# A two-block model on one core: where ScalarE loads the logarithm's tables, who scales the last rows and columns, and the order of the side work

## The chip, the cores and the metric

The kernel runs on one core of a Trainium2 chip. The metric is the device time of one execution, in microseconds (us); before the change it is 1814.29 us, the median of three executions (1814.15 to 1815.69).

## What is computed

`reference()` runs two small transformers one after the other on 256 tokens of width 1024, batch 1, in fp32.

- The first has two layers. Layer 0 mixes with four heads of differential attention and four heads of a gated linear recurrence; layer 1 mixes with 16 heads of dilated attention. Each layer then has a layer norm ("ln1"), a feed-forward part of width 4096 with a squared relu, a second layer norm ("ln2"), and a gated embedding.
- The second has two layers on a main path (x, the output of the first) and on a context path (256 context tokens). Each layer has an RMS norm with a modulation, a mixer of three parts (gated linear attention, six heads of neighbourhood attention, six heads of sliding-window attention; both attentions of the main path see 512 keys, the context's 256), a gated residual, a second modulated RMS norm, and a SwiGLU of width 2816. The context path ends with the keys and values of layer 1.
- The last step is an RMS norm, and that is what the change touches at the end:

```python
def rms_norm_2(x, g):
    xf = x.astype(jnp.float32)
    y = xf * lax.rsqrt(jnp.mean(xf * xf, axis=-1, keepdims=True) + NORM_EPS)
    return (y * g.astype(jnp.float32)).astype(x.dtype)
...
    return rms_norm_2(x, final_norm)
```

## The kernel before

Activations lie transposed: 128 partitions by 8 chunks (`DC`) of the width, each chunk 256 tokens. A product of weights and activations is done in three matmuls per 128x128 block (L620 to L622, or L660 to L662 where weights are the moving side): every fp32 operand is split into a high part (rounded by ScalarE) and a low part (the rest, by VectorE), and high x high, high x low and low x high are summed in a bank of PSUM.

**Weights** come in three streams from one array in HBM, loaded by SyncE (L564). "main" has 410 tiles of 8 blocks for the first model and the main path, "side" has 110 tiles for the context path, "mod" has 96 tiles for the modulations (L820). Main and side tiles are cut into halves of 4 blocks (128x512). ScalarE makes the high part of a half tile (L586: `high<-ring`, `high_side<-ring_side`), VectorE the low part (L594). The side's ring has 4 halves.

**Order.** Every engine runs a fixed list of instructions. `Program.run` writes these lists in advance: each stage is a generator that yields the name of what it needs next, each lane (engine) keeps a clock of estimated times (`A_us`, `V_us`, ...), and of the parts that can go on first on a lane the one with the lowest rank is taken. TensorE's side and modulation parts have a rank that changes with time (`Pace`): `MOD_PLAN` and `SIDE_PLAN` are lists of (TensorE's clock in us, tiles that should be done by then), in between linear. A part that is behind its plan comes first (rank -3 or -6), one that is not comes after the main path (3 or 5) and fills the time in which the main path cannot go on. So the estimated costs and the two plans together set the order of everything.

**Tables on ScalarE.** `Program.tables` (L466) loads a set of activation tables when the next function isn't in the set that is loaded by then: logarithm and exponential are in one set, tanh is in another with the exponential, silu in a third. Squares, copies and scalings need none. A reciprocal root is Ln and then Exp (`rstd`, L868: the load at L470, Ln at L874, Exp at L878).

**Norms.** `scalar_layer_norm` (L1317) squares eight centred chunks (L1322), TensorE sums them over partitions (L1312), then comes `rstd`. In the second model `scalar_square_sums` (L1877) squares each chunk behind its last residual (L1871 on VectorE, squares at L1887), VectorE adds the squares (L1898), TensorE averages over partitions (L1909), and `scalar_rstd` follows. This second form is used on the main path for the feed-forward norms of both layers, for the mixer's norm of layer 1 and for the last norm, and on the context path for the two norms behind its first.

**The end.** `vector_final` (L2528) makes y in eight VectorE instructions, one for each chunk: X times the norm's weight (a column) times the reciprocal root (L2532). `sync_stores` (L2536) stores each chunk, 128 KB, when it is made (L2540).

**Softmax.** A unit is one head; it has two rows of scores (the two halves of the queries). VectorE adds the bias and takes the row's extreme (L1038), ScalarE takes the exponential and its sum (L1107), VectorE inverts the sums (L1072) and scales both rows (`vector_normalise`, L1078), TensorE turns them (`tensor_turns`, L980), VectorE or ScalarE copies the turned blocks (L1058), TensorE multiplies by the values (L1005). Rows have up to 256 columns in the first model (`odd_scores`; `da_scores` of the differential attention aside), 256 in the context (`c_scores`), 512 on the main path (`x_scores` in layer 0, `x_late_T` in layer 1).

Of the kernel before, what the change touches and what calls it, by code (L numbers as in the profile page):

```python
# [16 lines left out]
P = 128  # L17
# [255 lines left out]
def A_us(n):  # L273
    return 0.2 + n / 1200.0


def V_us(n):
    return 0.15 + n / 960.0
# [6 lines left out]
class Program:  # L285
    def __init__(self, nc, ctx, io):
# [17 lines left out]
        self.s_turned_a = signal("turned_copied_scalar")  # L304
# [659 lines left out]
def tensor_turns(k, w, tag, units, banks, Tt):  # L964
    nc, T = k.nc, k.T
    for i, u in enumerate(units):
        blocks = blocks_of(u, Tt[i % len(Tt)])
        for j in range(len(u["rows"])):
            T.wait_ge(k.s_scaled, (yield tag, "scaled", i, j))
# [92 lines left out]
def vector_normalise(k, w, tag, u, i, Tt):  # L1062
# [9 lines left out]
    nc.vector.reciprocal(rd[:, 0:n_rows], den[:, 0:n_rows]).then_inc(*V.tick(k.s_vec, 0.17))  # L1072
    V.wait_ge(k.s_vec, V.last)
    h = n_rows // 2 if u["diff"] else n_rows
    for j in range(h):
        _, _, cols, to, _, _, _ = rows[j]
        names = [] if u["diff"] else [(tag, "scaled", i, j)]
        nc.vector.tensor_scalar(T_[:, to:to + cols], T_[:, to:to + cols], rd[:, j:j + 1], None, ALU.mult).then_inc(  # L1078
            *V.tick(k.s_scaled, V_us(cols) * 0.8, *names))
# [12 lines left out]

def scalar_attention(k, w, tag, units, Tt, PT):
# [3 lines left out]
    for step in range(n + lag):  # L1097
        if step < n:
# [218 lines left out]
def scalar_layer_norm(k, w, tag, b, layer):  # L1317
    nc, A = k.nc, k.A
    for i in range(DC):
# [3 lines left out]
            *A.tick(k.s_squares, A_us(SEQ), (tag, "square", i)))  # L1323
    A.wait_ge(k.s_sums, (yield tag, "summed", DC - 1))
# [552 lines left out]
def scalar_square_sums(k, w, prod, tag):  # L1877

    nc, A = k.nc, k.A
    for i in range(DC):  # L1880
# [4 lines left out]
        else:  # L1885
            j = k.sq_of[tag, i] = yield from w.sq.take(A, (tag, "added", i))
            nc.scalar.activation(w.SQ[:, j, 0:SEQ], w.X[:, i, :], ACT.Square).then_inc(  # L1887
                *A.tick(k.s_squares, A_us(SEQ), (tag, "square", i)))

# [638 lines left out]
def vector_final(k, w):  # L2528
    nc, V = k.nc, k.V
    for i in range(DC):  # L2530
        V.wait_ge(k.s_rstd, (yield ("final",), "rstd"))
        nc.vector.scalar_tensor_tensor(k.y[:, i, :], w.X[:, i, :], k.col("final", i), w.RS[:, 0, 0:SEQ], ALU.mult,  # L2532
                                       ALU.mult).then_inc(*V.tick(k.s_vec, V_us(SEQ), ("y", i)))


def sync_stores(k):  # L2536
    nc, D_ = k.nc, k.D
    for i in range(DC):
        D_.wait_ge(k.s_vec, (yield "y", i))
        nc.sync.dma_start(k.io["out"][:, i, :], k.y[:, i, :]).then_inc(*D_.tick(k.s_out, 0.1, by=16, later=2.0))  # L2540
    D_.wait_ge(k.s_out, D_.last)
# [80 lines left out]
MOD_PLAN = [(0, 0), (115, 20), (195, 32), (390, 76), (435, MOD_TILES)]  # L2622
SIDE_PLAN = [(430, 0), (560, 11), (715, 23), (790, 42), (970, 51), (1035, 72), (1215, 81), (1290, 98), (1375, 100), (1495, 110)]


def emit(k):
# [120 lines left out]
    k.add(V, vector_final(k, x), 0)  # L2747
    k.add(D_, sync_stores(k), 0)
# [231 lines left out]
```

## Time and profile before

| | |
|---|---|
| median of three executions | 1814.29 us (1814.15 to 1815.69) |
| the profiled execution, its own time | 1817.45 us |
| its span (first to last instruction) | 1816.2 us |
| instructions | 37913 |
| mean granted clock of TensorE | 0.991 of full speed |

The profile comes from one more execution, 3.2 us above the median; its span is 1.25 us shorter than its own time. Times in the trace are counted from the span's start. PE is TensorE's matmuls, PEld its weight loads, DVE VectorE, ACT ScalarE, POOL GpSimd, SPq SyncE's queue that issues DMAs. Matmuls overlap one another, so their durations say less than the distance of their starts.

### The profile page before, as it was taken

What the parts mean: (1) busy time and instruction counts of PE and PEld (TensorE: products, weight loads), DVE (VectorE), ACT (ScalarE), POOL (GpSimd) and SP (SyncE); (2) the same over time, 40 slices, a digit from 0 to 9 for tenths busy, and PEclk for the clock granted to TensorE, in tenths of its full rate; (3) what the DMA queues carried; (4) which work ended last, traced back from release to release, by engine and by line L of the source; (5) the groups of instructions that cost most, each with busy time, mean ns of one, the idle gap of its engine ahead of it and who ended that gap; (6) DMA issues with size and microseconds to landing.
All of it is one profiled execution on the core that took longest, in us unless ns stands there. A gap on an engine that the chain in (4) does not pass through costs nothing.

```text
span 1816.2 us, 37913 instructions
## 1 busy us (share of the span) xinstructions
PE 1777.4 (98%) x14762; PEld 1656.5 (91%) x14762; DVE 1352.7 (74%) x2948; ACT 1090.3 (60%) x2317; POOL 78.5 (4%) x81
## 2 busy tenths in 40 slices
PE   9999999999999999999999999999999999999997
PEld 7787999988989999999989998899999998689997
DVE  7676757578888876886687777886876888877766
ACT  5674646477666655665675656565664765565554
POOL 0001100020001000000020010100000000100000
PEclk9999999999999999999999999999999999999999
DMA  9959766886444645456555554456666543245663
GB/s 361 352 163 340 257 189 222 286 318 197 146 139 145 187 145 175 129 168 184 172 158 163 159 152 127 123 164 185 186 189 188 164 146 117 77 140 181 187 183 112
DMA packets 168610, 334.83 MB, mean 184 GB/s; under 512 B 19296, under 2 KB 21152, under 8 KB 168304
## 3 DMA queue, kind: packets, MB, share of 16 engines
q1 hardware_dynamic: 166752, 327.30, 56.6%
q0 software_dynamic: 1680, 5.11, 1.0%
q8 instruction: 117, 1.92, 0.4%
q14 instruction: 61, 0.50, 0.1%
HBM read 331.29 MB, written 1.05 MB: 183 GB/s over the span
## 4 chain that ended last, share of the span: by engine, by line
PE 92%; DVE 3%; DMA 2%; ACT 2%; issue 1%; SPq 1%; ACTq 0%; DVEq 0%
PE bank L620 25%; PE bank L621 24%; PE bank L622 24%; PE bank L1005 2%; PE bank L955 2%; PE bank L660 2%; PE bank L662 2%; PE bank L661 2%; PE bank L820 2%; PE bank L980 2%; PE bank L1312 1%; DMA ring_side<-in_stream 1%; DMA ring<-in_stream 1%; DVE Xx L1345 1%; PE bank L1990 1%
## 5 line engine op out<-in xcount | busy, mean ns | idle before, releaser
L594 DVE TENSOR_TENSOR low<-ring,high 128x512 fp32r<-128x512 f32 x820 | 556.2, 691 | 187.3 <-ACT high L586 176.6
L586 ACT CAST high<-ring 128x512 fp32r<-128x512 f32 x820 | 503.2, 619 | 311.5 <-PE bank L622 252.6
L620 PE MATMUL bank<-XHx,high 128*128 128x256 f32 x1720 | 502.2, 292 | 9.9 <-DVE XLx L1350 2.4
L621 PE MATMUL bank<-XLx,high 128*128 128x256 f32 x1720 | 485.6, 282 | 0.0
L622 PE MATMUL bank<-XHx,low 128*128 128x256 f32 x1720 | 484.9, 282 | 0.0
L620 PEld LDWEIGHTS bank<-XHx,high 128*128 128x128 f32 x1720 | 326.2, 190 | 31.7 <-issue 12.8
L621 PEld LDWEIGHTS bank<-XLx,high 128*128 128x128 f32 x1720 | 326.9, 190 | 0.9
L622 PEld LDWEIGHTS bank<-XHx,low 128*128 128x128 f32 x1720 | 326.7, 190 | 0.0
L586 ACT CAST high_side<-ring_side 128x512 fp32r<-128x512 f32 x220 | 135.2, 618 | 78.8 <-DMA ring_side<-in_stream 73.8
L594 DVE TENSOR_TENSOR low_side<-ring_side,high_side 128x512 fp32r<-128x512 f32 x220 | 152.5, 702 | 37.5 <-ACT high_side L586 32.6
L620 PE MATMUL bank<-XHc,high_side 128*128 128x256 f32 x608 | 176.6, 291 | 3.0 <-DVE low_side L594 3.0
L621 PE MATMUL bank<-XLc,high_side 128*128 128x256 f32 x608 | 172.1, 283 | 0.0
L622 PE MATMUL bank<-XHc,low_side 128*128 128x256 f32 x608 | 172.0, 283 | 0.0
L620 PE MATMUL bank<-hidden_high,high 128*128 128x256 f32 x512 | 145.1, 283 | 0.0
L622 PE MATMUL bank<-hidden_high,low 128*128 128x256 f32 x512 | 143.3, 280 | 0.0
L621 PE MATMUL bank<-hidden_low,high 128*128 128x256 f32 x512 | 142.9, 279 | 0.0
L620 PEld LDWEIGHTS bank<-XHc,high_side 128*128 128x128 f32 x608 | 115.9, 191 | 9.1 <-issue 4.4
L621 PEld LDWEIGHTS bank<-XLc,high_side 128*128 128x128 f32 x608 | 116.2, 191 | 0.6
L622 PEld LDWEIGHTS bank<-XHc,low_side 128*128 128x128 f32 x608 | 116.3, 191 | 0.0
L620 PE MATMUL bank<-x_early_high,high 128*128 128x258 f32 x376 | 107.8, 287 | 1.8 <-DVE low L594 1.8
L622 PE MATMUL bank<-x_early_high,low 128*128 128x258 f32 x376 | 106.0, 282 | 0.0
L621 PE MATMUL bank<-x_early_low,high 128*128 128x258 f32 x376 | 105.9, 282 | 0.0
(471 smaller groups left out, 3590.7 us busy)
## 6 DMA issues: line engine op xcount, KB each, us to landing
ring<-in_stream SPq DMA_DIRECT2D x820, 256.0 KB, 3.0
ring_side<-in_stream SPq DMA_DIRECT2D x220, 256.0 KB, 2.9
ring_mod<-in_stream SPq DMA_DIRECT2D x96, 512.0 KB, 7.7
x_nb<-in_rpb POOLq DMA_DIRECT2D x6, 256.0 KB, 3.6
x_late_NB<-in_rpb POOLq DMA_DIRECT2D x6, 256.0 KB, 3.2
Xx<-in_x SPq DMA_DIRECT2D x2, 512.0 KB, 5.8
Xc<-in_ctx SPq DMA_DIRECT2D x1, 1024.0 KB, 5.9
out<-y SPq DMA_DIRECT2D x8, 128.0 KB, 2.0
```

Of the source, the lines that this page charges most:

```text
L586: nc.scalar.copy(st.high[:, j % st.n_split, :], st.ring[:, j % st.n_ring, :]).then_inc(*A.tick(st.s_high, A_us(st.tb * P), (st.name, "high ...
L594: nc.vector.tensor_tensor(st.low[:, j % st.n_ring, :], st.ring[:, j % st.n_ring, :], st.high[:, j % st.n_split, :].bitcast(F32), ALU.subtr ...
L620: nc.tensor.matmul(out, wh, xh, start=(i == 0), stop=False)
L621: nc.tensor.matmul(out, wh, xl, start=False, stop=False)
L622: m = nc.tensor.matmul(out, wl, xh, start=False, stop=(c == ks[-1]))
L660: nc.tensor.matmul(bank[:, 0:n], xh, wh, start=(c == 0), stop=False)
L661: nc.tensor.matmul(bank[:, 0:n], xl, wh, start=False, stop=False)
L662: m = nc.tensor.matmul(bank[:, 0:n], xh, wl, start=False, stop=(c == DC - 1))
L820: m = nc.tensor.matmul(k.bank[b][32 * j:32 * j + 32, 0:256], k.cs[:, c, :], raw[:, 256 * j:256 * j + 256], start=(c == 0), stop=(c == DC - 1),
L955: m = nc.tensor.matmul(k.bank[k.bank_of[tag, "scores", i, g]][:, o:o + cols], q, kk, start=(o == 0), stop=True, skip_group_check=True)
L980: m = nc.tensor.transpose(k.bank[b][:, o:o + P], src, k.c["ident"][:, :])
L1005: m = nc.tensor.matmul(k.bank[b][u["at"], q0:SEQ], u["v"](kt), PTi[:, kt, q0:SEQ], start=(kt == 0), stop=(kt == keys - 1), skip_group_chec ...
```

## The change

Four edits. (1) In `scalar_layer_norm` and `scalar_square_sums` the call that loads the logarithm's tables stands behind the last square and no longer only in `rstd`, which still has its own call. (2) The last norm's weights are multiplied in place into X by ScalarE, one chunk at a time (`scalar_final`, rank 2); VectorE makes y of two chunks in one instruction, X times the reciprocal root, and a store takes two chunks. (3) In every attention but the differential one the last of a unit's two rows is scaled by ScalarE; the reciprocal gets a name of its own to be waited for, and TensorE's turns wait for both engines. (4) `MOD_PLAN` and `SIDE_PLAN` have other points.

```diff
@@ Program.__init__
-        self.s_turned_a = signal("turned_copied_scalar")
+        self.s_turned_a, self.s_scaled_a = signal("turned_copied_scalar"), signal("scaled_scalar")
@@ tensor_turns
-            T.wait_ge(k.s_scaled, (yield tag, "scaled", i, j))
+            T.wait_for((yield tag, "scaled", i, j))
@@ vector_normalise
-    nc.vector.reciprocal(rd[:, 0:n_rows], den[:, 0:n_rows]).then_inc(*V.tick(k.s_vec, 0.17))
+    nc.vector.reciprocal(rd[:, 0:n_rows], den[:, 0:n_rows]).then_inc(*V.tick(k.s_vec, 0.17, (tag, "reciprocal", i)))
     V.wait_ge(k.s_vec, V.last)
     h = n_rows // 2 if u["diff"] else n_rows
     for j in range(h):
+        if scaled_on_scalar(u, j):
+            continue
...
+def scaled_on_scalar(u, j):
+    return not u["diff"] and j == len(u["rows"]) - 1
+
+def scalar_normalise(k, w, tag, u, i, Tt):
+    nc, A = k.nc, k.A
+    _, _, rd, _ = columns_of(w, i, len(Tt))
+    for j, (_, _, cols, to, _, _, _) in enumerate(u["rows"]):
+        if scaled_on_scalar(u, j):
+            row = Tt[i % len(Tt)][:, to:to + cols]
+            A.wait_ge(k.s_vec, (yield tag, "reciprocal", i))
+            nc.scalar.activation(row, row, ACT.Copy, scale=rd[:, j:j + 1]).then_inc(
+                *A.tick(k.s_scaled_a, A_us(cols), (tag, "scaled", i, j)))
@@ scalar_attention
     for step in range(n + lag):
+        if step >= lag:
+            yield from scalar_normalise(k, w, tag, units[step - lag], step - lag, Tt)
         if step < n:
@@ scalar_layer_norm, behind the loop of squares
+    k.tables("ln")
     A.wait_ge(k.s_sums, (yield tag, "summed", DC - 1))
@@ scalar_square_sums, behind the loop of squares
+    k.tables("ln")
@@ vector_final
+    rs = w.RS[:, 0, 0:SEQ].unsqueeze(1).to_broadcast([P, 2, SEQ])
+    for i in range(0, DC, 2):
+        V.wait_ge(k.s_rstd, (yield ("final",), "rstd"))
+        V.wait_ge(k.s_act, (yield "gained", i + 1))
+        nc.vector.tensor_tensor(k.y[:, i:i + 2, :], w.X[:, i:i + 2, :], rs, ALU.mult).then_inc(
+            *V.tick(k.s_vec, V_us(2 * SEQ), ("y", i + 1)))
+
+def scalar_final(k, w):
+    nc, A = k.nc, k.A
     for i in range(DC):
-        V.wait_ge(k.s_rstd, (yield ("final",), "rstd"))
-        nc.vector.scalar_tensor_tensor(k.y[:, i, :], w.X[:, i, :], k.col("final", i), w.RS[:, 0, 0:SEQ], ALU.mult,
-                                       ALU.mult).then_inc(*V.tick(k.s_vec, V_us(SEQ), ("y", i)))
+        A.wait_ge(k.s_squares, (yield ("final",), "square", i))
+        nc.scalar.activation(w.X[:, i, :], w.X[:, i, :], ACT.Copy, scale=k.col("final", i)).then_inc(
+            *A.tick(k.s_act, A_us(SEQ), ("gained", i)))
@@ sync_stores
-    for i in range(DC):
-        D_.wait_ge(k.s_vec, (yield "y", i))
-        nc.sync.dma_start(k.io["out"][:, i, :], k.y[:, i, :]).then_inc(*D_.tick(k.s_out, 0.1, by=16, later=2.0))
+    for i in range(0, DC, 2):
+        D_.wait_ge(k.s_vec, (yield "y", i + 1))
+        nc.sync.dma_start(k.io["out"][:, i:i + 2, :], k.y[:, i:i + 2, :]).then_inc(*D_.tick(k.s_out, 0.1, by=16, later=2.0))
@@ plans
-MOD_PLAN = [(0, 0), (115, 20), (195, 32), (390, 76), (435, MOD_TILES)]
-SIDE_PLAN = [(430, 0), (560, 11), (715, 23), (790, 42), (970, 51), (1035, 72), (1215, 81), (1290, 98), (1375, 100), (1495, 110)]
+MOD_PLAN = [(0, 0), (115, 20), (195, 32), (390, 76), (460, MOD_TILES)]
+SIDE_PLAN = [(425, 0), (570, 11), (735, 23), (760, 46), (970, 61), (1015, 77), (1215, 81), (1285, 98), (1340, 100), (1515, 110)]
@@ emit
     k.add(V, vector_final(k, x), 0)
+    k.add(A, scalar_final(k, x), 2)
```

## Rows read from the trace of the kernel before

**Rows 1.** The page's first part: busy time, share of the span, instructions of each engine.
```profile
PE 1777.4 (98%) x14762; PEld 1656.5 (91%) x14762; DVE 1352.7 (74%) x2948; ACT 1090.3 (60%) x2317; POOL 78.5 (4%) x81
```

**Rows 2.** Stretches: length, busy us (count) by engine, granted clock, DMA share, GB/s.
```profile
185.00:300.00 115.00, 115.00 (x996) 114.16 (x987) 77.20 (x138) 65.38 (x131) 2.08 (x2) 1.00 0.67 208
900.00:960.00 60.00, 55.15 (x380) 51.74 (x379) 45.74 (x94) 42.57 (x86) 13.57 (x14) 0.91 0.49 149
960.00:1080.00 120.00, 120.00 (x1088) 115.84 (x1088) 86.74 (x180) 73.46 (x146) 5.82 (x6) 1.00 0.54 162
1180.00:1210.00 30.00, 27.03 (x211) 26.39 (x211) 25.62 (x56) 21.45 (x43) 0.00 (x0) 0.94 0.52 156
1530.00:1610.00 80.00, 75.83 (x534) 59.90 (x533) 64.22 (x156) 47.23 (x113) 7.97 (x8) 0.96 0.30 91
```

**Rows 3.** Waits of TensorE over the span: us in total, times, longest.
```profile
PE bank L620 <- DVE low_side L594: 4.4, 3, 2.5
...
PE bank L660 <- DVE low L594: 2.0, 1, 2.0
...
PE bank L1005 <- DVE odd_scores L1078: 0.8, 1, 0.8
PE bank L1005 <- DVE x_late_T L1078: 0.7, 1, 0.7
```

**Rows 4.** ScalarE's timeline at the end: start, us, instruction, idle before.
```profile
1806.33 0.42 ACT L1887 ACTIVATE SQx<-Xx 128x256 f32<-128x256 f32 x1 [1.68 <-DVE Xx L1871]
1807.98 1.28 ACT L470 ACT_TABLE_LOAD   x1 [1.24 <-PE bank L1909]
1809.28 0.47 ACT L874 ACTIVATE RSx<-bank,c_cols 128x256 f32<-128x256 f32 x1
1809.78 0.42 ACT L878 ACTIVATE RSx<-RSx 128x256 f32<-128x256 f32 x1
```

**Rows 5.** Timeline of VectorE and of SyncE's queue at the end.
```profile
1810.23 3.25 DVE L2532 SCALAR_TENSOR_TENSOR y<-Xx,par,RSx 128x256 f32<-128x256 f32 x8 [3.03 <-ACT RSx L878]
...
1810.74 3.78 SPq L2540 DMA_DIRECT2D out<-y  x8
```

**Rows 6.** Line 2540, the eight stores of 128 KB: issue to landing.
```profile
DMA to landing us min/median/max: 1.9/2.0/2.1
```

**Rows 7.** The page's DMA issues: count, KB each, median us to landing.
```profile
ring<-in_stream SPq DMA_DIRECT2D x820, 256.0 KB, 3.0
```

**Rows 8.** Groups of instructions by shape: count, busy us, mean ns, idle before.
```profile
L1107 ACT ACTIVATE x_late_T<-x_late_T,smallx 128x512 f32<-128x512 f32 x24 | 17.1, 716 | 5.3 <-DVE smallx L1038 5.3
...
L1078 DVE TENSOR_SCALAR x_scores<-x_scores,smallx 128x512 f32<-128x512 f32 x24 | 10.6, 484 | 0.4
...
L1338 DVE TENSOR_TENSOR Xx<-Xx,bank 128x512 f32<-128x512 f32 x16 | 9.9, 683 | 1.4 <-PE bank L1298 1.4
...
L698 ACT ACTIVATE x_early_high<-Xx,gsx 128x256 fp32r<-128x256 f32 x16 | 8.1, 509 | 1.4 <-PE bank L622 1.1
```

**Rows 9.** ScalarE's timeline at ln2 of layer 1.
```profile
902.96 0.42 ACT L1322 ACTIVATE SQx<-Xx 128x256 f32<-128x256 f32 x1 [0.72 <-PE bank L1312]
...
904.51 1.28 ACT L470 ACT_TABLE_LOAD   x1 [0.50 <-PE bank L1312]
```

**Rows 10.** TensorE's timeline at the first product behind that norm.
```profile
909.12 0.36 PE L620 MATMUL bank<-XHx,high 128*128 128x256 f32 x1 [0.83 <-DVE XLx L1350]
```

**Rows 11.** ScalarE's timeline at the second model's first feed-forward norm.
```profile
1191.52 0.42 ACT L1887 ACTIVATE SQx<-Xx 128x256 f32<-128x256 f32 x1
1192.99 0.39 ACT L2409 ACTIVATE TMPc<-bank 128x256 f32<-128x256 f32 x1 [1.06 <-issue]
1194.09 1.28 ACT L470 ACT_TABLE_LOAD   x1 [0.71 <-PE bank L1909]
```

**Rows 12.** Stretches of `ring_side` alone: VectorE busy (count), ScalarE busy (count of half tiles).
```profile
0.00:1015.00 1015.00, 87.94 (x129) 79.49 (x130) 0.99 0.64 209
1080.00:1180.00 100.00, 16.63 (x22) 13.55 (x22) 1.00 0.42 125
```

## The prediction

> **What bounds the kernel now.** I read the page's first part, then TensorE's waits, then the stretches, and then the timelines where the edits sit. TensorE is busy for 1777.4 of 1816.2 us [rows 1]; nothing in the change takes a matmul away. In a plain stretch of products it has no idle time at all, 996 matmuls in 115 us, 0.1155 us each [rows 2]. So time can come only from the 38.8 us in which TensorE is not busy: from what lies behind its last matmul, and from stalls. The stretches show where stalls are: 4.85 us of 60 idle at 900 to 960, 2.97 of 30 at 1180 to 1210, 4.17 of 80 at 1530 to 1610; in these three the mean granted clock is 0.91, 0.94 and 0.96, that is, TensorE ran for a part of them at 1.2 instead of 2.4 GHz after it had been idle [rows 2]. The waits that matter here end with a low part of a half tile (4.4 us in three, 2.0 in one) or with a scaled row of scores (0.8 and 0.7) [rows 3].
>
> **The end.** ScalarE's last square starts at 1806.33 and ends at 1806.75. Then ScalarE idles 1.24 us until the sum over partitions is there, loads the tables for 1.28 us from 1807.98, and has Ln at 1809.28 and Exp to 1810.20 [rows 4]. After the change the load follows the square: 1806.76 to 1808.04, which is 0.06 behind the sum. But the weights of the eighth chunk (0.509 us, the form of L698, a copy with a column as scale [rows 8]) are ready before the sum in the planner's estimate and go in between; the other seven lie in ScalarE's idle time of 1.68 us before each square [rows 4] and cost nothing. If that cover were gone, each would delay by 0.43. Rows that follow one another overlap by 0.08 (eight y of 0.48 take 3.25, so they start 0.40 apart [rows 5]), so Ln starts at 1808.47 instead of 1809.28: **-0.8** (at best -1.2, without the weights in between).
>
> The load costs 1.28 us here, and what follows it starts 0.02 later [rows 4]. The Trainium skill, "ScalarE: Activation LUTs", section "What ACT_TABLE_LOAD costs", counts 1283 ns for the load and 1380 ns for a drain, 2.66 us for each switch. By that figure up to 1.4 us more would be hidden, and the whole sum below would be some 1.4 us larger; the load agrees with the trace, the drain shows in no row here, and the rows decide.
>
> From Exp's end at 1810.20 to the last store's landing it is 5.9 us now: eight y in 3.25, while SyncE issues a store each 0.47 us (eight in 3.78), later than they are made, so that the last issue starts at 1814.1 [rows 5] and lands 2.0 us later [rows 6]. After it: four y of 128x512, each like L1338's 0.683 us [rows 8], 0.60 apart, so 2.48; the queue now keeps up; and a store of 256 KB. That landing is not in the trace: the same queue's store of 128 KB takes 2.0 us [rows 6], a load of 256 KB among others 3.0 [rows 7]. I take 2.3, since a store alone at the end is nearer to the first. 0.06 + 2.48 + 2.3 = 4.84: **-1.0** (-1.4 with 2.0, -0.4 with 3.0). What is late next is the last of the four y and its store's landing. VectorE's new wait for the weights ends before Exp does.
>
> **The norms in between.** A load moves only where other tables were loaded by then; these are two norms of the main path besides the last, and one of the context (TensorE does not wait for that). At ln2 of layer 1 the last square ends at 903.38 and the load starts at 904.51, at the sum [rows 9]: 1.1 us earlier afterwards. TensorE first waits 0.83 us behind it at 909.12 [rows 10], with context products as filler before; later chunks come at VectorE's pace. **-0.8**, between 0 (the filler is used up as well) and -1.1. At the first feed-forward norm the last square ends at 1191.94, the load would end at 1193.22, before the sum at 1194.09, so all 1.28 us go. Of the 2.97 us that TensorE idles around it [rows 2], 2.5 are its longest wait for a context half tile [rows 3], whose low part VectorE makes behind its first work for the norm. But a tanh of the context stands at 1192.99 [rows 11]. If it still comes in between, tanh's tables are loaded again and then the logarithm's: 1191.94 + 3 x 1.28 + 0.39 = 1196.2, where Ln now starts at 1195.4, that is +0.8. I take half of the gain, **-0.6**, between -1.3 and +0.8.
>
> **The softmax row.** One scaling in each unit leaves VectorE: 16 in the first model, 12 in the context and 24 on the main path, the last 512 wide. At 512 columns the scaling takes 0.484 us on VectorE, 0.40 with the overlap; ScalarE has 0.716 for a row of that size with a column operand [rows 8]. Both rows now run at once: done 0.72 us behind the reciprocal instead of 0.88, and VectorE is free 0.40 earlier for the next row or half tile. While TensorE has other products this is worth nothing. It counts where TensorE waits for such a row or for a low part behind it: the 2.0, 0.8 and 0.7 us [rows 3], each shorter by 0.40: **-1.2**. Best case: all 12 units of layer 1's attention, 4.8 us. ScalarE's 0.72 us lie in its idle time there (47 of 80 us busy [rows 2]); the wait for the reciprocal blocks the high parts behind it, but the exponentials that follow wait for VectorE anyway.
>
> **The plans.** No matmul is added; each part of TensorE's work only moves. The modulations get 25 us longer, the context path is asked for 12 tiles more by 1015 (77 where 130 half tiles, 65 tiles, were begun in the trace [rows 12]). At 960 to 1080, where this work is forced already, TensorE never idles [rows 2], so I take **0**. Bounds: the idle time of the two norm stretches less what is counted above, about -6; two more waits like the longest one, +5.
>
> **Sum.** -0.8 - 1.0 - 0.8 - 0.6 - 1.2 + 0 = -4.4 us. The durations are of an execution that took 1817.45 us by itself (span 1816.2), 3.2 above the median; the differences are applied to the median: 1814.29 - 4.4 = **1809.9 us**, -0.24%. A measurement of this kernel can tell about 0.2%, 3.6 us, from no change, so the forecast lies just on the far side of that.
>
> **Rivals.**
> - *Only the end counts.* Everything in between is hidden by filler, since TensorE is busy anyway: -1.8 us, 1812.5, no change by the bound. For it: TensorE has filler at all three places but layer 1's attention. Against it: waits of 0.7 to 2.5 us stand there in spite of it.
> - *The early load does not stay.* A tanh between square and Ln takes it back at the middle norms: -4.4 + 0.8 + 0.6 + 0.8 = -2.2, 1812.1. The tanh at 1192.99 speaks for it at one norm; at 904 nothing but squares and copies stood between.
> - *The row on ScalarE is late.* If ScalarE is in an operation of 0.72 us when the reciprocal comes, the row is done at 1.43 us instead of 0.88; over layer 1's 12 units without filler +6.6 us: -4.4 + 1.2 + 6.6 = +3.4, 1817.7. Against it: ScalarE's idle share there. The Trainium skill, "ScalarE: Activation LUTs", section "Rules for kernel authors", gives multiplications to VectorE, not ScalarE, which speaks against both moves of the change; the trace agrees on the single instruction (0.716 us for an operation of that size against 0.484 [rows 8]).
> - *Slower: the context path's work is missing later.* Pulled ahead by 12 tiles before 1015, it is no longer there as filler in layer 0's attention (1080 to 1180), where 22 half tiles were begun [rows 12]. A half tile is 12 matmuls, 1.39 us. If six are missing there, 8.3 us outweigh the gain and put the time above +3.6; with nine it is 1814.29 - 4.4 + 12.5 = 1822.4. Against it: 66 half tiles are still left at 77 of 110 tiles, unless a context norm blocks them just then.
>
> **How the numbers follow.** Forecast 0.50, only the end 0.22, load taken back 0.06, late row 0.06, missing filler 0.16. The first is faster by over 0.2%, the next three lie within 0.2%, the last is slower: 0.50, 0.34, 0.16. The two signs' cases do not balance, so the forecast's own range, 1804 (with the plans' best bound) to 1811, stands beside the whole one: 1804 to 1818 (past the late row), which leaves out most of the slow case and the sum of all best cases, under 2 in 10.
>
> **What would show it.** Right: the last table load follows the last square at once, with one scaling row between it and Ln; four stores, the last landing about 4.8 us behind Exp; the load at the other two norms before the sum; TensorE's waits for `low` and scaled rows in 1530 to 1610 shorter; total idle down by some 3 us. Wrong: more table loads at L470 than before, scaling rows on ScalarE that start over 0.5 us behind the reciprocal, or idle time on TensorE in 1080 to 1210 that was not there.

## The result, and the profile after

The changed kernel takes 1802.22 us (median of three executions, 1801.48 to 1804.89) where the kernel before takes 1814.29. The ratio is 0.9933 with a 95% interval of 0.9918 to 0.9948: faster by 0.67%, 12.1 us. The forecast was 4.4 us, and 1804 the lower end of its range. In a second set of executions (`after_again`) it took 1800.11 us, ratio 0.9917 (0.9904 to 0.9930). The sign was right and the size was not. (One execution of `u_tables` below took 3449.37 us and is left out of its ratio.)

The first part of the page again, against [rows 1]. The profiled execution took 1804.89 us by itself, its span is 1803.6, so 12.6 less than before:

```profile
PE 1769.1 (98%) x14762; PEld 1651.6 (92%) x14762; DVE 1332.6 (74%) x2892; ACT 1123.0 (62%) x2379; POOL 78.2 (4%) x81
```

TensorE runs the same 14762 matmuls and is busy for 8.3 us less. The edits take no work away from a matmul, so a part of the 12.6 us must be clock. The stretches show it. First the kernel before, cut the same way for every kernel below (stretch, length, busy us and count of PE, PEld, DVE, ACT and POOL, the granted clock, DMA share, GB/s; the last row adds up all eight stretches from 0 to 1790 us):

```profile
0.00:60.00 60.00, 55.58 (x421) 44.35 (x422) 44.18 (x142) 34.77 (x86) 3.31 (x9) 0.97 0.99 364
...
880.00:980.00 100.00, 95.15 (x724) 91.28 (x723) 77.75 (x158) 69.64 (x144) 13.57 (x14) 0.95 0.52 157
...
1180.00:1230.00 50.00, 47.03 (x380) 46.39 (x380) 40.33 (x83) 32.15 (x64) 0.00 (x0) 0.97 0.56 166
...
1500.00:1630.00 130.00, 124.06 (x957) 105.72 (x957) 105.59 (x248) 76.82 (x180) 8.43 (x9) 0.96 0.36 108
...
sum 1790.00, PE 1761.37 PEld 1641.08 DVE 1339.27 ACT 1082.12 POOL 78.55; mean PE 220.17 PEld 205.13 DVE 167.41 ACT 135.26 POOL 9.82
```

And the changed kernel:

```profile
0.00:60.00 60.00, 55.71 (x424) 44.68 (x425) 44.27 (x142) 35.08 (x86) 3.30 (x9) 0.97 1.00 369
...
880.00:980.00 100.00, 97.48 (x782) 96.16 (x781) 73.26 (x146) 68.45 (x135) 14.52 (x14) 0.98 0.57 174
...
1180.00:1230.00 50.00, 48.04 (x395) 47.02 (x394) 40.76 (x84) 32.90 (x65) 0.00 (x0) 1.00 0.58 172
...
1500.00:1630.00 130.00, 125.50 (x945) 109.22 (x945) 98.76 (x223) 85.01 (x192) 7.95 (x8) 0.99 0.40 117
...
sum 1790.00, PE 1763.77 PEld 1646.86 DVE 1327.33 ACT 1118.14 POOL 78.20; mean PE 220.47 PEld 205.86 DVE 165.92 ACT 139.77 POOL 9.77
```

TensorE's clock has two levels, 1.2 and 2.4 GHz, so a mean of 0.95 over 100 us says that it stood at the lower one for 10 of them. Summed over the four stretches (the others read 1.00) that is 3.6 + 10 + 3 + 10.4 = 27 us before and 3.6 + 4 + 0 + 2.6 = 10 us after. What the lower level does to the work shows in the kernel before, just behind the wait of 2.0 us at L660 [rows 3]: these matmuls start 0.23 us apart, and 0.43 when the clock has fallen.

```profile
1555.93 0.40 PE L661 MATMUL bank<-high,XLx 128*128 128x512 f32 x1
1556.16 0.39 PE L662 MATMUL bank<-low,XHx 128*128 128x512 f32 x1
...
1556.67 0.63 PE L661 MATMUL bank<-high,XLx 128*128 128x512 f32 x1
1557.10 0.63 PE L662 MATMUL bank<-low,XHx 128*128 128x512 f32 x1
```

So each such microsecond costs half of one where TensorE works through it, and less where it waits anyway: at most 13.5 before, 5.1 after. Of the 12.6 us that gives

- clock: 27 to 10 us at the low level, **-8.4**;
- TensorE idle up to 1790 us: 28.6 (1790 - 1761.37) to 26.2, **-2.4**;
- the end behind TensorE's last matmul: 8.20 to 6.76 us, **-1.4**.

The second and third are the terms that the forecast worked with. The first had no term.

This is one pair of executions, and the clock's share in it is on the high side. The traced execution of the kernel before has a granted clock of 0.991. In the 61 executions of it beside the experiments below the clock runs from 0.989 to 0.996, and the time goes with it: the slowest, 1820.74 us, has 0.989, the fastest, 1811.14 us, 0.995. What is missing of 1 in the mean clock, times the span, is what the clock costs at most. The 61 have 0.9929 in the mean, the changed kernel 0.9957 in the first set and 0.9970 in the second. By that the clock is some 5 of the 12.1 us, and some 7 of the 14.7 in the second set.

The waits of TensorE from 100 to 1790 us (total, times, longest), against [rows 3]:

```profile
PE bank L620 <- DVE low_side L594: 4.7, 6, 2.1
...
PE bank L620 <- DVE low L594: 1.8, 1, 1.8
PE bank L980 <- issue: 1.5, 1, 1.5
```

The waits for a context half tile are no shorter in total, 4.7 for 4.4 us; there are six for three, and the longest is 2.1 instead of 2.5. The wait of 2.0 us at L660 in layer 1's attention is gone.

The end, against [rows 4] and [rows 5]: first ScalarE's timeline, then VectorE's and that of SyncE's queue, then the page's row of DMA issues for the stores (how many, KB each, median us to landing).

```profile
1795.19 0.42 ACT L1908 ACTIVATE SQx<-Xx 128x256 f32<-128x256 f32 x1 [1.14 <-DVE Xx L1892]
1795.63 1.28 ACT L470 ACT_TABLE_LOAD   x1
1796.92 0.51 ACT L2564 ACTIVATE Xx<-Xx,par 128x256 f32<-128x256 f32 x1
1797.34 0.45 ACT L874 ACTIVATE RSx<-bank,c_cols 128x256 f32<-128x256 f32 x1
1797.82 0.42 ACT L878 ACTIVATE RSx<-RSx 128x256 f32<-128x256 f32 x1
```

```profile
1798.27 2.50 DVE L2556 TENSOR_TENSOR y<-Xx,RSx 128x512 f32<-128x512 f32 x4 [2.20 <-ACT RSx L878]
...
1798.99 2.14 SPq L2572 DMA_DIRECT2D out<-y  x4
```

```profile
out<-y SPq DMA_DIRECT2D x4, 256.0 KB, 2.7
```

It is built as forecast: the load follows the last square, the weights of the eighth chunk stand between it and Ln, and from the square's end to Ln it is 1.73 us (1795.61 to 1797.34) instead of 2.53. From Exp's end (1798.24) to the span's end it is 5.4 us instead of 6.0.

### The profile page after: what moved, and what is told of

The parts are those of the page before. It is cut to its first block, busy times and chain, and to the rows that moved or that the text cites. A ratio compares the mean times of both kernels' runs of the same rounds, so it can differ in the third digit from the quotient of the medians.

```text
span 1803.6 us, 37901 instructions
## 1 busy us (share of the span) xinstructions
PE 1769.1 (98%) x14762; PEld 1651.6 (92%) x14762; DVE 1332.6 (74%) x2892; ACT 1123.0 (62%) x2379; POOL 78.2 (4%) x81
## 4 chain that ended last, share of the span: by engine, by line
PE 90%; DVE 3%; ACT 3%; DMA 2%; issue 1%; SPq 1%; ACTq 0%; DVEq 0%
PE bank L620 25%; PE bank L621 24%; PE bank L622 24%; PE bank L1005 2%; PE bank L955 2%; PE bank L660 2%; PE bank L820 2%; PE bank L661 2%; PE bank L662 2%; PE bank L980 2%; DMA ring_side<-in_stream 1%; PE bank L1332 1%; DVE Xx L1366 1%; ACT L470 1%; DMA ring<-in_stream 1%
## 5 line engine op out<-in xcount | busy, mean ns | idle before, releaser
L620 PE MATMUL bank<-XHx,high 128*128 128x256 f32 x1720 | 498.5, 290 | 6.8 <-ACT TMPc L791 2.2
L620 PEld LDWEIGHTS bank<-XHx,high 128*128 128x128 f32 x1720 | 324.7, 189 | 25.8 <-issue 10.9
L620 PE MATMUL bank<-XHc,high_side 128*128 128x256 f32 x608 | 179.7, 296 | 4.5 <-DVE low_side L594 3.9
L620 PE MATMUL bank<-hidden_high,high 128*128 128x256 f32 x512 | 145.7, 285 | 0.0
L620 PEld LDWEIGHTS bank<-XHc,high_side 128*128 128x128 f32 x608 | 115.9, 191 | 12.8 <-issue 5.3
L620 PE MATMUL bank<-x_early_high,high 128*128 128x258 f32 x376 | 107.5, 286 | 1.8 <-DVE low L594 1.8
```

The source lines that it names most:

```text
L620: nc.tensor.matmul(out, wh, xh, start=(i == 0), stop=False)
```

## The experiments

Sixteen kernels besides the changed one itself, which ran once more; each time is a median, and each ratio is against the kernel before on the same chip, with its 95% interval.

### 1. One part undone, the order planned anew

Each is the changed kernel with one part taken back.

```diff
# u_plans
-SIDE_PLAN = [(425, 0), (570, 11), (735, 23), (760, 46), (970, 61), (1015, 77), ...]
+SIDE_PLAN = [(430, 0), (560, 11), (715, 23), (790, 42), (970, 51), (1035, 72), ...]
# u_softmax, in scaled_on_scalar
-    return not u["diff"] and j == len(u["rows"]) - 1
+    return False
# u_tables, in scalar_layer_norm and scalar_square_sums
-    k.tables("ln")
# u_final
-    k.add(A, scalar_final(k, x), 2)
```

(`u_plans` has the old `MOD_PLAN` too, `u_final` the old `vector_final`.)

> All of the change but the two plans, which are those of before. Theory: the 7.7 us beyond the forecast came from TensorE running at 2.4 instead of 1.2 GHz where it used to stall around 895 to 960 us, because the context path now has work there; with the old plans these low stretches (some 10 us) and about 4 us of idle time come back, and the time is 1807 to 1811. Rival: edits 1 to 3 gave it; the time stays at 1801 to 1804 and the low stretches stay away.

Measured: 1822.96 us, ratio 1.0036 (1.0023 to 1.0048). Slower than the kernel before, with three of the four edits in.

> All of the change but the softmax rows: VectorE scales both. Theory: layer 1's attention (1524 to 1576) gets its waits for low parts back, and with them 3.4 to 6.8 us at 1.2 GHz: 1804 to 1808. Rival: the plans alone cured that stage, and the time is 1801 to 1804 with no low stretch there.

Measured: 1819.48 us, 1.0014 (1.0005 to 1.0023). Slower too.

> All of the change but the early table loads: each load waits for the sum again. Theory (the forecast's terms): +1.2 at the end, +0 to +2.4 at two norms: 1803 to 1806, with one table load between the last sum and Ln. Rival: the early loads are what keeps TensorE from idling at the norms, so low stretches come back at 890 to 930 or at 1195: over 1807.

Measured: 1807.15 us, 0.9951 (0.9937 to 0.9964).

> All of the change but the last norm's weights and the stores of two chunks: eight y on VectorE with the weights in them, eight stores. Theory: the end gets back 1.0 us of y and stores and loses the scaling row ahead of Ln (0.4): 1802.5 to 1803.5. Rival: nothing at the end matters beyond the table load: within 0.3 us of 1802.2.

Measured: 1801.21 us, 0.9919 (0.9905 to 0.9932), no slower than the changed kernel. The list of matmuls is the same in both, so this one is a clean comparison: the weights on ScalarE and y of two chunks in one instruction are worth nothing that can be measured. Its end is 6.98 us against 6.76, so of the 1.44 us that the end gained, 1.22 come from the tables alone.

Two of four expectations are off by some 12 us, and in the same way: without the plans, or without the softmax edit, the whole gain is lost. But the planner puts thousands of TensorE's lines in another place in `u_plans` and `u_softmax`, and over a thousand in `u_tables`, and so none of these three measures its edit alone.

### 2. The plans alone, and the order moved by a trifle

`o_plans` is the kernel before with both new plans. For the nudges, one figure of the planner's estimate moves by 2 ns; no work changes, but a quarter and more of TensorE's lines come in another order.

```diff
# n_after: the changed kernel; n_before: the kernel before; n_oplans: o_plans
 def V_us(n):
-    return 0.15 + n / 960.0
+    return 0.152 + n / 960.0
# n2_after: the changed kernel
+    return 0.148 + n / 960.0
```

> The kernel before with the new plans alone. Theory 'the plans carry the gain' (the context's tiles pulled ahead feed TensorE behind 895 to 960 whatever the other edits are): 1804 to 1809 us, with TensorE's low-clock time down from 27 us by 10 or more and no drop at 911 and 956. Rival 'the plans fit one schedule only' (they were set for the order that the other three edits make; with the old order the due times fall elsewhere): 1813 to 1822 us, drops still near 950 and 1556.

Measured: 1825.55 us, 1.0051 (1.0038 to 1.0063). The plans alone lose 10 us, more than either theory had. Two of its waits of TensorE:

```profile
PE bank L620 <- DVE low_side L594: 7.9, 3, 3.6
PE bank L620 <- DVE XLx L1350: 4.3, 4, 3.4
```

The 3.4 us stand at 592.06 us, at the first product behind a layer norm of the first model, the 3.6 at 951.32. At the first the main path is late (the reading of half tiles begun says 325 main ones at 660 us where the changed kernel has 332), and no context product runs in between.

> The changed kernel with one number of the planner's estimate moved by a trifle (0.150 to 0.152 us for a VectorE instruction), which re-orders thousands of lines but changes no work. Theory 'a schedule property' (the gain sits in where stalls and drops fall, and any new order scatters them): off the changed kernel's time by 3 us or more, likely slower, up to 1815, with drops at other places. Rival 'the edits themselves carry the gain': within 2 us of the changed kernel.

Measured: 1805.31 us, 0.9947 (0.9934 to 0.9961), 2.5 to 5.4 us behind the changed kernel (0.9933 and 0.9917). Most of the gain stays, though the loss is more than the 2 us that the edits' theory allowed. The nudge the other way leaves none of it:

> The changed kernel with the planner's VectorE figure moved the other way (0.150 to 0.148 us), no work changed. Theory 'the edits, ordered anyhow, carry most of the gain': within 4 us of the changed kernel, as the first nudge was (0.9947). Rival 'the gain is luck of one order': 1808 to 1820.

Measured: 1821.00 us, 1.0038 (1.0025 to 1.0051). A change of 2 ns in an estimate takes the whole gain away and more. Its waits:

```profile
PE bank L620 <- ACT e L1495: 6.8, 5, 2.4
PE bank L620 <- DVE low_side L594: 6.0, 4, 2.9
PE bank L620 <- DVE XLx L1371: 3.4, 1, 3.4
```

All edits are in, and the wait of 3.4 us behind the same layer norm as in `o_plans` is back, now at 586 us.

> The kernel before with the first nudge (0.150 to 0.152 us). Theory as above: within 4 us of the kernel before, 1811 to 1818. Rival: it falls as near to the changed kernel as to the kernel before, below 1809, or above 1820.

Measured: 1820.98 us, 1.0032 (1.0020 to 1.0044): 6 us slower for the nudge that `n_after` has. That is over 1820, as the rival had it.

> The kernel before with the new plans alone, and the first nudge. Theory 'the new plans without the softmax edit lose 10 us because the main path is slower between 520 and 600 us and stands at its norm without context products': again over 1820, with TensorE waiting over 2 us near 592 and 951. Rival 'luck of one order': 1805 to 1818.

Measured: 1831.54 us, 1.0089 (1.0076 to 1.0102). This is as the theory had it: TensorE waits 2.72 us at 588 and 5.70 us at 950. `u_softmax`, which has the new plans and lacks the softmax edit too, has the same two waits, 3.44 us at 592 and 4.65 us at 950.

> The changed kernel unaltered, on the chip of the three nudged ones: 1801.5 to 1805, ratio 0.992 to 0.995 to the kernel before; its profile shows whether the drop behind the stall at 1601 us (there in the first trace, not behind the same stall of the kernel without the new y) comes each time.

Measured: 1800.11 us, 0.9917 (0.9904 to 0.9930). The drop behind the stall at about 1600 us is absent from this trace, with the same list of instructions and the same 1.8 us of idle time: whether the clock falls behind such a stall differs from execution to execution.

So the kernel before and the changed one are each a good order among worse neighbours: three orders with all edits in span 1800 to 1821 us, two orders of the kernel before 1815 to 1821. What this scatter doesn't say is what the edits do when the order stands still.

### 3. Idle time filled with matmuls

If the clock is a term of its own, then it can be bought without shortening any wait. `b_fill` is the kernel before with 34 matmuls of 128x128, whose results nobody reads, in front of nine waits; the planner does not know of them, so the rest of every list stays. (It counts 68 records, two for each. Lines are shifted: L634 is L620 of before.)

```diff
+FILL_TILE = {('side', 105): 6, ('side', 174): 10, ('main', 689): 7}
+def filler(k, spare, n, alone):
+    for _ in range(n):
+        k.nc.tensor.matmul(spare, k.keep[:, 0:P], k.keep[:, 0:P], start=alone, stop=alone)
 def weights(k, st, blocks, ...):
     if o == 0:
-        k.T.wait_ge(st.s_low, (yield st.name, "low", tile))
+        mark = yield st.name, "low", tile
+        if spare is not None:
+            filler(k, spare, FILL_TILE.get((st.name, tile), 0), alone)
+        k.T.wait_ge(st.s_low, mark)
```

(The other 11 stand in front of six waits for a chunk of the norms at 908 and 950 us, in `products`. `spare` is the last quarter of the product's own bank.)

> The kernel before with 34 idle-time matmuls of 128x128 (0.21 us each) added on TensorE in front of nine waits at 908, 949, 950 to 955, 1196 and 1612 us; the order of everything else stays. Theory 'the clock is the main term' (TensorE falls to 1.2 GHz behind idle time, and each such stretch of 3.4 us costs 1.7): the drops at 911 (6.8 us), 956, 1198 and 1615 go or shrink, 10 to 17 us less at the low clock, and the time falls by 5 to 8.5 us against the kernel before, though no wait got shorter. Rival 'only the waits count' (the gain came from shorter waits and a shorter end): no change within 1 us, or up to 2 us slower where a fill delays the product behind it.

Measured: 1810.23 us, 0.9967 (0.9954 to 0.9979): 5.4 us faster by the medians, as the clock theory had it. The five executions have a granted clock of 0.998 or 0.999, the nine of the kernel before beside them 0.990 to 0.993. The fills and the stretches:

```profile
L605 PE MATMUL bank<-keep x68: 270/275/377, 909.0 to 1607.4; 128*128 128x128 f32 x68
```

```profile
0.00:60.00 60.00, 55.53 (x425) 44.67 (x426) 44.20 (x142) 34.99 (x87) 3.30 (x9) 0.97 1.00 369
...
880.00:980.00 100.00, 96.44 (x779) 93.36 (x778) 78.36 (x160) 70.85 (x146) 12.84 (x14) 1.00 0.53 161
...
1180.00:1230.00 50.00, 49.08 (x405) 48.05 (x404) 40.26 (x83) 32.87 (x66) 0.00 (x0) 1.00 0.56 168
...
1500.00:1630.00 130.00, 125.74 (x996) 109.63 (x995) 107.46 (x249) 78.55 (x183) 8.51 (x8) 1.00 0.38 117
```

Outside of the first 60 us the clock reads 1.00 everywhere: 3.6 us at the low level instead of 27. That would be 11.7 us. Some of it goes back, since a part of the fills ran where TensorE would have had work: 68 records 0.11 us apart are 7.6 us, and the idle time up to 1790 us falls only by 3.9 (28.6 to 24.7), so I estimate 3.7 us. Four of the five falls after the first 60 us stood at waits that were filled. The fifth, 6.8 us at the low level, stood behind the wait of 1.95 us in layer 1's attention, which was not filled; it stayed away in this execution by itself. The falls of the clock follow idle time of TensorE, and filling the idle time takes them away: that is shown at the four. The same in the better orders brings nothing that can be measured, where less is left:

> The changed kernel without the new weights and y at the end, with 23 such matmuls in front of three waits at 971, 1195 and 1598 us, the rest in the same order. Theory 'the clock': the drop at 974 goes and none comes at 1197 or 1600; 1.7 to 3.4 us faster than the same kernel without them (1801.2 in its run), so about 1798.5. Rival 'only the waits count': 1801 to 1803.

Measured: 1800.65 us, 0.9919 (0.9905 to 0.9932), the ratio of `u_final` without the fills; in the profiled execution 3.4 us at the low level for 6.8.

> The changed kernel with 23 idle-time matmuls in front of its waits at 971, 1195 and 1600 us, the rest in the same order. By the clock: the drop at 974 (and the one at 1603 where it comes) go, 1.7 to 3.4 us faster than the changed kernel, 1797 to 1799.5; if the fills delay as much as they save, 1799.5 to 1802.

Measured: 1800.08 us, 0.9922 (0.9908 to 0.9935), as the changed kernel without them. Neither beats it, and both miss what was expected by the clock.

### 4. The order held, the edits changed in execution alone

These separate the order from the edits. In `r_softmax`, `r_tables` and `r_all` the planner plans the changed kernel as it is, so that every engine's list stays, but the edit is undone in what is emitted: the row's scaling stands on VectorE behind the reciprocal, the table load behind the sum. `r_all` undoes all three edits: the work of the kernel before in the order of the changed one.

```diff
# r_softmax: in vector_normalise, without V.tick
         if scaled_on_scalar(u, j):
+            k.s_scaled.n += 1
+            k.on_vector[tag, i, j] = k.s_scaled.n
+            nc.vector.tensor_scalar(T_[:, to:to + cols], T_[:, to:to + cols], rd[:, j:j + 1], None, ALU.mult).then_inc(
+                k.s_scaled.sem, 1)
             continue
...
# and in scalar_normalise
-            nc.scalar.activation(row, row, ACT.Copy, scale=rd[:, j:j + 1]).then_inc(...)
+            A.spend(A_us(cols))
+            k.marks[tag, "scaled", i, j] = Mark(k.s_scaled, k.on_vector[tag, i, j], A.clock + A.lag)
# r_tables: planned at the square, loaded where Ln needs it
-    k.tables("ln")
+    k.tables("ln", later=True)
```

> The changed kernel in its own order, planned as it is, but the last softmax row of each unit is scaled on VectorE again, in line behind the reciprocal. Theory 'the order carries the gain': 1801 to 1804, at most 3 us above the changed kernel (1800.1 in its last run; my 1.2 us for this edit). Rival 'the scaling itself carries it' (each of 52 units 0.3 to 0.4 us later, more where TensorE waits): 1808 to 1816.

Measured: 1802.09 us, 0.9933 (0.9921 to 0.9946).

> The changed kernel in its own order with the logarithm's tables loaded behind the sum again at every norm. Theory 'the order': 1801 to 1804, with 0.8 to 1.3 us at the end (as the runs' ends 8.20 and 6.98 us say) and under 1.4 at the two norms between, as the forecast had it. Rival 'the early load matters in the norms between': 1805 to 1812.

Measured: 1805.22 us, 0.9948 (0.9936 to 0.9961), 3 to 5 us behind the changed kernel; more than the first theory had, at the edge of the second. The place shows at the first feed-forward norm of the second model. The changed kernel, ScalarE and then TensorE:

```profile
1191.61 0.42 ACT L1908 ACTIVATE SQx<-Xx 128x256 f32<-128x256 f32 x1
1192.04 1.28 ACT L470 ACT_TABLE_LOAD   x1
1194.40 0.48 ACT L874 ACTIVATE RSx<-bank,c_cols 128x256 f32<-128x256 f32 x1 [1.08 <-PE bank L1931]
...
1197.30 0.39 PE L620 MATMUL bank<-XHc,high_side 128*128 128x256 f32 x1 [1.50 <-DVE low_side L594]
```

`r_tables` (L474 and L877 are L470 and L874 here):

```profile
1192.70 1.28 ACT L474 ACT_TABLE_LOAD   x1 [2.37 <-PE bank L1934]
1193.99 0.47 ACT L877 ACTIVATE RSx<-bank,c_cols 128x256 f32<-128x256 f32 x1
...
1196.89 0.58 PE L623 MATMUL bank<-XHc,high_side 128*128 128x256 f32 x1 [2.78 <-DVE low_side L597]
```

```profile
1180.00:1230.00 50.00, 47.22 (x374) 46.96 (x373) 39.28 (x80) 31.74 (x64) 0.00 (x0) 0.93 0.53 161
```

The last row is the stretch around it. TensorE's wait is 2.78 instead of 1.50 us: longer by 1.28, the table load to the hundredth. The Trainium skill, "ScalarE: Activation LUTs", section "What ACT_TABLE_LOAD costs", counts 2.66 us for a switch; the wait grew by 1.28, so its drain does not show here either. And behind the longer wait the clock falls (0.93 over these 50 us, 7 us at the low level, where the changed kernel has 1.00). So in that execution the load of 1.28 us costs up to 1.3 + 3.5 us, the larger part in clock. The second part is not fixed: behind the same wait of 2.78 us in `r_all`, next, the low level lasts 3 us.

> The changed kernel's order and plans with all three edits undone in execution (tables behind the sum, rows on VectorE, the end as before): the work of the kernel before in the changed kernel's order. Theory 'the order carries the gain': 1802 to 1807, that is, 8 us or more under the kernel before with nothing but another order. Rival 'the edits carry it': 1810 to 1820.

Measured: 1807.02 us, 0.9960 (0.9947 to 0.9972). The work of the kernel before is 7.3 us faster in the other order, with no instruction of it shorter. Its stretches:

```profile
0.00:60.00 60.00, 56.26 (x440) 44.55 (x444) 44.66 (x146) 36.26 (x89) 3.31 (x9) 1.00 1.00 373
...
880.00:980.00 100.00, 97.46 (x787) 96.32 (x786) 74.01 (x149) 66.75 (x135) 15.28 (x14) 0.98 0.57 175
...
1180.00:1230.00 50.00, 47.22 (x384) 46.96 (x383) 39.95 (x82) 32.34 (x64) 0.00 (x0) 0.97 0.55 167
...
1500.00:1630.00 130.00, 123.92 (x934) 107.84 (x934) 101.55 (x233) 77.33 (x179) 7.97 (x8) 0.99 0.37 115
...
sum 1790.00, PE 1761.67 PEld 1646.36 DVE 1341.69 ACT 1090.76 POOL 79.24; mean PE 220.21 PEld 205.79 DVE 167.71 ACT 136.35 POOL 9.91
```

TensorE idles for 28.3 us up to 1790, as before the change (28.6); but at the low clock it is for 4 + 3 + 2.6 = 9.6 us instead of 27. The order took hardly any idle time away; with it the clock fell less. How much of the 7.3 us that is, two traces don't say. Their spans differ by 10.5 us, of which the clock is up to 8.7. But the trace of the kernel before is one of low clock, as said above, and 1.8 of the 8.7 come from the first 60 us, where TensorE's list is the same in both kernels. By the mean granted clocks, 0.9958 in these five executions and 0.9934 in the nine of the kernel before beside them, it is some 4 of the 7.3.

Last, the counterpart: the order and plans of the kernel before, and the three edits in execution alone (`q_all`; the scaling stands on ScalarE's list where VectorE had planned it, the load behind the last square, the end as changed).

```diff
 # in vector_normalise, with the planner's clock of VectorE as before
+            V.clock += V_us(cols) * 0.8
...
+            k.A.wait_ge(k.s_vec, k.marks[tag, "reciprocal", i])
+            nc.scalar.activation(row, row, ACT.Copy, scale=rd[:, j:j + 1]).then_inc(k.s_scaled_a.sem, 1)
```

> The kernel before in its own order and plans, with the three edits made in execution alone (tables behind the last square, last softmax rows on ScalarE at the place where VectorE had them in the plan, weights and y at the end). Theory 'the sum was right for the edits, the order was left out': 4.4 us under the kernel before (1809 to 1812 where that takes 1814.5), the end 8.2 to 6.8 us. Here one table load more stands at the feed-forward norm at 1192 us, where a tanh takes the early one back, so up to 1.3 us of it may be missing. Rival 'the edits need the new order': 1813 to 1823, as with the old plans re-planned.

Measured: 1811.40 us (1809.08 to 1815.34, 12 executions), 0.9989 (0.9979 to 0.9999). In the order for which the sum was made, the edits are worth 2.0 us, between 0.2 and 3.8; the forecast's 4.4 is a little above that. Its stretches, and then the first row of its page and of `r_all`'s:

```profile
0.00:60.00 60.00, 55.49 (x425) 44.62 (x426) 44.27 (x142) 35.12 (x87) 3.30 (x9) 0.97 1.00 370
...
880.00:980.00 100.00, 95.12 (x750) 91.70 (x749) 78.27 (x161) 71.61 (x147) 12.83 (x14) 0.98 0.53 163
...
1180.00:1230.00 50.00, 46.31 (x380) 45.34 (x380) 40.12 (x83) 34.80 (x66) 0.00 (x0) 1.00 0.58 167
...
1500.00:1630.00 130.00, 124.67 (x976) 108.30 (x975) 101.94 (x238) 85.54 (x195) 8.48 (x8) 0.99 0.38 116
```

```profile
PE 1771.9 (98%) x14762; PEld 1652.6 (91%) x14762; DVE 1334.8 (74%) x2892; ACT 1121.1 (62%) x2379; POOL 78.3 (4%) x81
```

```profile
PE 1767.7 (98%) x14762; PEld 1651.8 (91%) x14762; DVE 1348.1 (75%) x2948; ACT 1094.2 (61%) x2317; POOL 79.2 (4%) x81
```

This execution, in the old order, is at the low level for 3.6 + 4 + 2.6 = 10 us, about as long as that of `r_all` in the new one (9.6). Yet with the same 14762 matmuls TensorE is busy for 4.2 us longer than in `r_all`. So the clock is not all that the new order gives; what the rest is was not found.

The load taken back at the feed-forward norm shows as expected:

```profile
1190.13 2.57 ACT L474 ACT_TABLE_LOAD   x2
1192.71 0.38 ACT L2438 ACTIVATE TMPc<-bank 128x256 f32<-128x256 f32 x1
1193.11 1.28 ACT L474 ACT_TABLE_LOAD   x1
...
1197.38 0.36 PE L623 MATMUL bank<-XHc,high_side 128*128 128x256 f32 x1 [2.94 <-DVE low_side L597]
```

The same wait in the kernel before:

```profile
1198.68 0.55 PE L620 MATMUL bank<-XHc,high_side 128*128 128x256 f32 x1 [2.46 <-DVE low_side L594]
```

The logarithm's tables at 1190.13, tanh's at once behind them, the logarithm's again at 1193.11, and TensorE waits 2.94 us where the kernel before waits 2.46. Behind this longer wait the clock stayed up (1.00 from 1180 to 1230).

## Why the prediction was wrong

The step that failed is the one on the plans: "At 960 to 1080, where this work is forced already, TensorE never idles [rows 2], so I take **0**". It looked for what the plans do in one stretch, and priced them in idle time alone. The plans and the other edits' estimates together set a new order, and that order by itself is worth 7.3 us (`r_all`), more than the whole forecast, while the idle time stays. Some 4 us of it are clock by the mean of the executions, and more in the traces, where 27 us at the low level become 9.6; the rest is open. The clock was named in the first part (0.91, 0.94 and 0.96 in the three stretches of [rows 2]) and then given no term in the sum. Its price stood in those rows: a mean of 0.91 over 60 us is 10.8 us at 1.2 GHz, of which up to half is lost, 5.4; with 1.8 and 3.2 from the other two that makes 10.4 us. With it the plans' best bound would have been some 16 us, not 6, and the range would have held the result. That the sign came out right is in part luck: with all four edits in and an estimate moved by 2 ns, `n2_after` is slower than the kernel before.

Point by point:

- **The end**, -1.8 forecast, -1.44 measured. The tables were right: 2.53 to 1.73 us between square and Ln is -0.80, as forecast. y and stores were too large at -1.0: it is 6.0 to 5.4, -0.6, because a store of 256 KB lands in 2.7 us and not in 2.3; the bound of 3.0 was the nearer one. The 0.4 us that the eighth weights cost ahead of Ln come off that, and so the second edit is worth about 0.2 us by the ends (6.98 and 6.76), nothing that the times show.
- **ln2 of layer 1**, -0.8 forecast: nothing. In `q_all` TensorE is busy for 95.12 of the 100 us from 880, where the kernel before is for 95.15; in `r_tables` it is for 97.73 and in the changed kernel for 97.48. The first wait of 0.83 us is gone in `q_all`, and four for the next chunks, 0.31 to 0.48 us each, take its place, where the kernel before has three of 0.18 to 0.40.
- **First feed-forward norm**, -0.6 forecast as half of a gain, with -1.3 and +0.8 as bounds. Each came in its order, by TensorE's wait: -1.28 in the new one, +0.48 of the 0.8 in the old one, where the tanh takes the load back.
- **The softmax row**, -1.2 forecast. Over 1500 to 1630 TensorE is busy for 125.50 us in the changed kernel and 124.81 in `r_softmax`, 124.67 in `q_all` and 124.06 before: 0.6 to 0.7 us. But in `u_final`, which has this edit and the changed kernel's order, it is for 124.85, so this is no clear gain. Of the waits named, the one of 2.0 us is 1.56 in `q_all`, shorter by the 0.40 forecast; those of 0.8 and 0.7 stay as they were. By the times of `r_softmax` it is between 0 and 3 us.
- **All edits together**, -4.4 forecast: -2.0 in the old order; in the new one `r_all` stands 4.9 to 7.8 us above the changed kernel (0.9960 against 0.9933 and 0.9917). The forecast lies between the two.

Of the rivals, "the context path's work is missing later" is a real mechanism at other places: in `o_plans`, which has the new plans without the other edits and is 10 us slower, TensorE waits 3.4 us at 592 and 3.6 at 951. In the changed kernel they don't arise, and 980 to 1180 keeps its 199.5 busy us of 200. What would have shown the forecast wrong, more table loads at L470, did come (44 for 42, so two more loads of 1.28 us on ScalarE), and the kernel was faster all the same.

What stays open: what the new order gives beside the clock, some 3 of its 7.3 us, was not found. Why the old plans with the three edits (1822.96) and the new plans without them (1825.55) are both slower than either kernel is only traced to where their waits stand, not to one decision of the planner. And whether the clock falls behind one given stall can't be foretold from these traces.

## What to carry to other kernels

Where a planner writes the order of all engines from estimates, an edit's forecast has two terms: what it is worth with the order held, which rows of the trace give to a few microseconds (4.4 forecast here, 2.0 measured in the old order), and what the new order does, which they don't give at all; here 2 to 7 us against a scatter of 20. Measure the first by changing the execution and not the plan, and nudge an estimate by a trifle to see the second before believing either. And give the low clock a term of its own: a microsecond at half speed costs up to half of one, it comes on top of the stall that it follows, and it is read from the granted clock of the stretch.

## What the runs showed of the hardware

- Filling idle time in front of nine waits with matmuls that nobody reads took the time at the low clock from 27 to 3.6 us (6.8 of it at a wait that was not filled) and made the kernel 0.33% faster, though TensorE had more to do.
- Executions of one and the same kernel differ by their clock: over 61 of the kernel before it is granted 0.989 to 0.996, and the times from 1820.74 to 1811.14 us go with it.
- The clock's fall does not follow a stall every time: behind the same 1.8 us at about 1600 us it fell in one execution of the changed kernel and did not in another; behind 2.0 us at 1552 in `b_fill` it did not, and behind 2.94 us at 1197 in `q_all` it did not, where 2.46 us at the same place of the kernel before were enough.
- A store of 256 KB at the end lands in 2.7 us where one of 128 KB takes 2.0 [rows 6], so halving their number gave back 0.7 of the 1.3 us by which the last store is issued sooner behind Exp (2.6 us instead of 3.9).
